# Where weight preparation, evictions and a few activations stand in the attention stretches of a two-block transformer kernel

## The chip, the cores and the metric

The kernel runs on one core of a Trainium2 chip. Its engines are TensorE (PE), VectorE (DVE), ScalarE (ACT), GpSimd (POOL) and the queue of SyncE (SP), which starts the weight loads. The metric is the device time of one execution in microseconds (us); lower is better.

## What is computed

A first block (gated sparse attention and forgetting attention on 256 tokens, merge, output, a gated embedding) and then two layers, each with a token mixer, attention over a memory of 256 rows, and a squared-ReLU MLP. All is float32. Cut to what matters:

```
proj = rmsnorm(x, g_pre) @ w_in                      # 256 x 3792, split into q, k, v, gates, indexer
att_a = dsa_branch(...)                              # indexer scores, top 64 keys, softmax
log_f = log_sigmoid(fb + b_forget)                   # the forget gate
att_b = fox_branch(qb, kb, vb, log_f)                # 8 heads, causal
out = (m_a * (att_a*silu(gate_a)) @ w_a + m_b * (att_b*silu(gate_b)) @ w_b) @ w_out
for i in range(2):                                   # layer 0: pool mixer, layer 1: MoBA mixer
    h = rms_norm(x) @ (w_in_pool if i == 0 else w_in_moba)
    tok = pool_mixer(h) if i == 0 else moba_mixer(h) # 12 heads, q and k normed per head and rotated
    mo = mem_cross_attention(h[..., -256:], mem_n)   # 4 heads
    x = x + concat(tok, mo) @ w_out[i]
    x = x + square(relu(rms_norm(x) @ w_ff1[i])) @ w_ff2[i]
```

With 256 tokens and blocks of 256 the MoBA mixer is plain causal attention.

## The kernel before

**Weights.** Every weight matrix is cut into units of 4 k-tiles of 128 rows by 512 columns (440 or 384 in the first projection), numbered through the program: `U_IN`, `U_MERGE`, ..., `U_POOL`, `U_OUT0`, `U_FF0`, `U_MOBA0`, `U_MOBA`, `U_OUT1`, `U_FF1`. I write POOL+5 for unit `U_POOL + 5`, MOBA+3 for `U_MOBA + 3`; `U_OUT1` is `U_MOBA + 8`. A unit is loaded by SP into one of two `raw` slots (four in the first projection); ACT rounds it into `w_hi` and DVE subtracts to get `w_lo` (L690 and L1090), both in a ring of four. The call `unit(u)` on ACT and on DVE prepares unit u + 3: ACT waits for its load and until PE has used unit u - 1. SP starts the load of unit v when `w_lo` of unit v - 2 is there.

**Products.** `product` (L1618) takes three matmuls for each k-tile and each of two token tiles (hi with hi, hi with lo, lo with hi), 24 for a whole unit; a k-tile is six. Two units make a block of 512 output columns in two PSUM banks. When both are done, `evac` copies the banks out, tile 0 on ACT and tile 1 on DVE (`block_done` is the wait for PE). The next block in the same banks waits for both copies (`banks_free`).

**Attention.** It is cut into steps n; each handles a pair of heads, the first four steps the indexer. Run 1 (steps 0 to 11, drained in 12 and 13) is the first block, which I call stage 1; run 2 (steps 12 and 13) is the memory attention of layer 0, stage 2; run 3 (steps 14 to 21, drained in 22 and 23) that of layer 1: two pairs of memory heads and six pairs of MoBA heads, stage 3. In step n PE does the scores of pair n (`logits`, L1760), transposes q and k of pair n + 1 (`qk_parts`, L1730), multiplies the values of pair n - 2 (`values`, L1814), then runs a piece of a dense product (`fill_of(n)`: a unit, two units or some k-tiles of one), then transposes the probabilities of pair n - 1 (`transposes`). ACT copies q and k (`copy_qk`), takes exponentials (`exps`), copies outputs and probabilities, and prepares `w_hi`; DVE takes maxima, normalises, subtracts (`out_lo`), copies probabilities (`copy_pt`, L1292) and prepares `w_lo`. `qk_parts(n)` waits for DVE's `copy_pt(n - 3)`, since both use one bank. The scores of a pair's first tile reuse the bank of the pair before.

**Order.** Each engine's program is written out by hand and runs in that order; tables name what fills which step (`IN_FILL`, `MOBA_FILL`, `OUT_FILL`) and when the squares for the head norms are taken (`SQUARES_AT`). A unit that is divided over steps is prepared by `late_unit` at the end of a step. GpSimd rotates q0, k0, q1, k1, q2, k2 in this order, each after its squares (`head_squares`, L1151 and L1152, on DVE), and `qk_parts` of a MoBA pair waits for its q and k.

## Time and profile before

| | |
|---|---|
| median of 3 runs | 851.4 us (850.99 to 852.76) |
| profiled execution | 850.99 us, span 849.1 us |
| PE busy | 820.9 us, 97% of the span |
| PE weight loads | 702.2 us, 83% |
| DVE busy | 528.5 us, 62% |
| ACT busy | 423.6 us, 50% |
| POOL busy | 117.3 us, 14% |
| data read | 138.86 MB, 165 GB/s over the span |

The chain that ended last lies on PE for 89% of the span, 54% of it the products of L1618 and 22% those of the MLP's first half (L1942). PE's busy time counts overlapping matmuls and modelled ends, so its idle pieces are what to look for; the view of waits names the engine whose work ended each of them, or "issue" where no single releaser shows. The span is the time between the first and last instruction of the profiled run; 1.9 us of its time lie outside.

### The profile page before, as it was taken

What the parts mean: (1) busy time and instruction counts of PE and PEld (TensorE: products, weight loads), DVE (VectorE), ACT (ScalarE), POOL (GpSimd) and SP (SyncE); (2) the same over time, 40 slices, a digit from 0 to 9 for tenths busy, and PEclk for the clock granted to TensorE, in tenths of its full rate; (3) what the DMA queues carried; (4) which work ended last, traced back from release to release, by engine and by line L of the source; (5) the groups of instructions that cost most, each with busy time, mean ns of one, the idle gap of its engine ahead of it and who ended that gap; (6) DMA issues with size and microseconds to landing.
All of it is one profiled execution on the core that took longest, in us unless ns stands there. A gap on an engine that the chain in (4) does not pass through costs nothing.

```text
span 849.1 us, 11701 instructions
## 1 busy us (share of the span) xinstructions
PE 820.9 (97%) x4506; PEld 702.2 (83%) x4506; DVE 528.5 (62%) x655; ACT 423.6 (50%) x620; POOL 117.3 (14%) x143
## 2 busy tenths in 40 slices
PE   6999999999999999999999999997989899999998
PEld 6998977778878767899999998875657799999996
DVE  5546988767586766565554455779774655445542
ACT  6446656554755555454444434545574544444440
POOL 2600300000030410030000000099500100000000
PEclk9999999999999999999999999999999999999999
DMA  8851452245646532555555555462122455555531
GB/s 316 295 180 39 149 192 106 103 158 200 247 152 220 195 131 69 198 182 176 188 197 197 176 180 189 161 208 77 52 98 100 156 192 198 173 178 193 198 148 50
DMA packets 76181, 140.42 MB, mean 165 GB/s; under 512 B 2888, under 2 KB 22544, under 8 KB 76144
## 3 DMA queue, kind: packets, MB, share of 16 engines
q1 hardware_dynamic: 74048, 134.03, 46.1%
q0 software_dynamic: 1936, 5.82, 2.0%
q8 instruction: 25, 0.41, 0.2%
q14 instruction: 12, 0.10, 0.0%
q10 hardware_dynamic: 160, 0.07, 0.0%
HBM read 138.86 MB, written 1.05 MB: 165 GB/s over the span
## 4 chain that ended last, share of the span: by engine, by line
PE 89%; ACT 4%; DVE 3%; issue 2%; DMA 1%; POOL 0%; SPq 0%; ACTq 0%; DVEq 0%
PE bank L1618 54%; PE bank L1942 22%; PE bank L1760 3%; PE bank L1678 2%; ACT w_hi L690 2%; PE bank L1814 2%; PE bank L1647 1%; DVE w_lo L1090 1%; PE bank L1730 1%; PE bank L1815 1%; PE bank L1632 1%; PE bank L1989 1%; PE bank L1790 1%; DMA raw<-in_w_ff 1%; DMA x<-in_x 1%
## 5 line engine op out<-in xcount | busy, mean ns | idle before, releaser
L1090 DVE TENSOR_TENSOR w_lo<-raw,w_hi 128x2048 fp32r<-128x2048 f32 (+2 forms) x69 | 155.3, 2254 | 63.3 <-ACT w_hi L690 62.9
L1495 DVE TENSOR_TENSOR w_lo<-raw,w_hi 128x2048 fp32r<-128x2048 f32 x48 | 110.2, 2295 | 91.6 <-ACT w_hi L1001 91.6
L690 ACT ACTIVATE w_hi<-raw 128x2048 fp32r<-128x2048 f32 (+2 forms) x69 | 129.9, 1884 | 67.1 <-PE bank L1618 41.6
L1618 PE MATMUL bank<-w_hi,b_hi 128*128 128x512 f32 x376 | 149.2, 397 | 0.1
L1618 PE MATMUL bank<-w_hi,a_hi 128*128 128x512 f32 (+2 forms) x376 | 146.9, 391 | 0.4 <-PE bank L1618 0.4
L1942 PE MATMUL bank<-a_hi,w_hi 128*128 128x256 f32 x512 | 145.4, 284 | 1.7 <-ACT tok L979 1.1
L1618 PE MATMUL bank<-w_lo,b_hi 128*128 128x512 f32 x376 | 146.6, 390 | 0.0
L1618 PE MATMUL bank<-w_hi,b_lo 128*128 128x512 f32 x376 | 146.5, 390 | 0.0
L1942 PE MATMUL bank<-a_lo,w_hi 128*128 128x256 f32 x512 | 144.9, 283 | 0.0
L1942 PE MATMUL bank<-a_hi,w_lo 128*128 128x256 f32 x512 | 144.9, 283 | 0.0
L1618 PE MATMUL bank<-w_hi,a_lo 128*128 128x512 f32 (+2 forms) x376 | 142.1, 378 | 0.0
L1618 PE MATMUL bank<-w_lo,a_hi 128*128 128x512 f32 (+2 forms) x376 | 141.7, 377 | 0.0
L1001 ACT ACTIVATE w_hi<-raw 128x2048 fp32r<-128x2048 f32 x48 | 92.2, 1922 | 98.5 <-PE bank L1618 64.7
L1942 PEld LDWEIGHTS bank<-a_hi,w_hi 128*128 128x128 f32 x512 | 98.2, 192 | 2.9 <-DVE w_lo L1090 1.5
L1942 PEld LDWEIGHTS bank<-a_lo,w_hi 128*128 128x128 f32 x512 | 98.2, 192 | 0.5
L1942 PEld LDWEIGHTS bank<-a_hi,w_lo 128*128 128x128 f32 x512 | 98.2, 192 | 0.0
L1618 PEld LDWEIGHTS bank<-w_hi,b_lo 128*128 128x128 f32 x376 | 70.6, 188 | 15.0
L1618 PEld LDWEIGHTS bank<-w_hi,b_hi 128*128 128x128 f32 x376 | 70.7, 188 | 14.2 <-DVE b_lo L1481 0.5
L1618 PEld LDWEIGHTS bank<-w_lo,b_hi 128*128 128x128 f32 x376 | 70.7, 188 | 13.5
L1618 PEld LDWEIGHTS bank<-w_hi,a_hi 128*128 128x128 f32 x376 | 70.7, 188 | 11.4 <-issue 1.8
L1618 PEld LDWEIGHTS bank<-w_hi,a_lo 128*128 128x128 f32 x376 | 70.6, 188 | 11.3
L1618 PEld LDWEIGHTS bank<-w_lo,a_hi 128*128 128x128 f32 x376 | 70.8, 188 | 10.5 <-issue 0.7
(244 smaller groups left out, 908.6 us busy)
## 6 DMA issues: line engine op xcount, KB each, us to landing
raw<-in_w_ff SPq DMA_DIRECT2D x64, 1024.0 KB, 5.1
raw<-in_w_in_moba SPq DMA_DIRECT2D x20, 512.0 KB, 4.3
raw<-in_w_merge SPq DMA_DIRECT2D x8, 1024.0 KB, 5.1
raw<-in_w_out SPq DMA_DIRECT2D x8, 1024.0 KB, 5.1
raw<-in_w_in SPq DMA_DIRECT2D x6, 880.0 KB, 7.5
m<-in_w_in SPq DMA_DIRECT2D x6, 880.0 KB, 7.1
raw<-in_w_mem_kv SPq DMA_DIRECT2D x4, 1024.0 KB, 5.2
raw<-in_w_ple_gate SPq DMA_DIRECT2D x4, 1024.0 KB, 4.9
```

The lines of the kernel that those rows point to most:

```text
L690: act.activation(w_hi[:, slot, 0:n], landing[land][:, 0:n], ACT.Copy).then_inc(hi_ready, 1)
L1001: act.activation(w_hi[:, (base + c) % RING, :], raw[:, (base + c) % RAW, :], ACT.Copy)\
L1090: dve.tensor_tensor(w_lo[:, v % RING, 0:n], landing[land_slot(v)][:, 0:n], w_hi[:, v % RING, 0:n].bitcast(F32), ALU.subtract).then_inc(lo_ ...
L1495: dve.tensor_tensor(w_lo[:, (base + c) % RING, :], raw[:, (base + c) % RAW, :], w_hi[:, (base + c) % RING, :].bitcast(F32), ALU.subtract). ...
L1618: ins = pe.matmul(banks[t][:, 0:n], xa[:, kt, ts], wa[:, slot, w], start=first and k == 0 and q == 0, stop=last and k == kts - 1 and q == 2)
L1632: ins = pe.matmul(banks[t][:, :], xa[:, k0 + k, ts], wa[:, u % RING, w], start=False, stop=k == 3 and q == 2)
L1647: ins = pe.matmul(banks[t][:, 0:n], xa[:, k0 + k, t * P:t * P + P], wa[:, u, k * n:k * n + n], start=k0 + k + q == 0, stop=k0 + k == D // ...
L1678: ins = pe.transpose(ps[:, kk * S + t * P:kk * S + t * P + P], src[:, t, (k + kk) * P:(k + kk) * P + P], ident[:])
L1730: ins = pe.transpose(b_io[:, i * S + t * P:i * S + t * P + P], cols[what][:, t], ident[:])
L1760: ins = pe.matmul(out, qT[:, t * P:t * P + P], k_of(n)[:, :, 0:w], start=True, stop=open_)
L1814: pe.matmul(out, v[:, 0], pT[0], start=True, stop=False)
L1942: ins = pe.matmul(b_hid[f][:, 0:S], wa[:, slot, w], xa[:, 4 * half_ + k, :], start=half_ + k + q == 0, stop=half_ == 1 and k == 3 and q == 2)
```

## The change

It moves work and adds or removes none. (1) In stage 1 the forget gate's Exp and Ln, and the dummy Exp that brings the table of Exp back, go from the ends of steps 0 and 2 to step 1, ahead of its unit. (2) On DVE a step's unit is now always prepared before the eviction of the block that the step ends; it was the other way for the second unit of a step and in stage 3. (3) In stage 2 units POOL+5 and POOL+6 are prepared before the two query copies (ACT) and before the first maxima (DVE), and PE's transposes and scores go in one k-tile earlier. (4) In stage 3 the dense part ends with MOBA+2, and the fills of steps 14 to 19 are MOBA+3 to MOBA+7 instead of MOBA+4 to MOBA+7; the squares of k1, q2 and k2 move with them. (5) `late_unit` prepares for a divided unit in the first of its steps, not in the last.

```
--- before.py
+++ after.py
@@ -146,7 +146,7 @@
     if n in BR_FILL:
         return [(U_BR + BR_FILL[n], B_BR + BR_FILL[n], 2, range(4))]
     if n in MOBA_FILL:
-        return [unit_of(U_MOBA + 4, B_MOBA + 2, *MOBA_FILL[n])]
+        return [unit_of(U_MOBA + 2, B_MOBA + 1, *MOBA_FILL[n])]
     if n in OUT_FILL:
         return [(U_OUT1, B_OUT1, 0, range(OUT_FILL[n], OUT_FILL[n] + 1))]
     return []
@@ -156,10 +156,10 @@
 MERGE_FILL = {6: (0, 1), 7: (2, 3), 8: (4,), 9: (5,), 10: (6,), 11: (7,)}
 BR_FILL = {12: 0, 13: 1}
 DRAIN = (12, 13, 22, 23)
-MOBA_FILL = {14: (0,), 15: (1,), 16: (2, range(0, 2)), 17: (2, range(2, 4)), 18: (3, range(0, 2)), 19: (3, range(2, 4))}
+MOBA_FILL = {14: (1,), 15: (2,), 16: (3,), 17: (4,), 18: (5, range(0, 2)), 19: (5, range(2, 4))}
 OUT_FILL = {20: 0, 21: 1, 22: 2, 23: 3}
 
-SQUARES_AT = {16: (("k2", B_MOBA + 2),)}
+SQUARES_AT = {15: (("k1", B_MOBA + 1), ("q2", B_MOBA + 1)), 17: (("k2", B_MOBA + 2),)}
 
 MOBA_BLOCKS = [(0, 3), (1, 9), (2, 4), (5, 6), (7, 8)]
 MOBA_AT = {piece: 256 * n for n, piece in enumerate(q for b in MOBA_BLOCKS for q in b)}
@@ -778,7 +778,7 @@
             def late_unit(n):
 
                 for u, k, half_, ks in fill_of(n):
-                    if 3 in ks and len(ks) < 4:
+                    if 0 in ks and len(ks) < 4:
                         unit(u)
 
             def copy_qk(n):
@@ -852,21 +852,20 @@
                     copy_qk(n + 1)
                 if n in run:
                     relus(n) if n < N_IDX else exps(n)
+                if n == 1:
+
+                    act.wait_ge(f_abs, 1)
+                    act.activation(fgt[:, 2], fgt[:, 1], ACT.Exp).then_inc(act_chain, 1)
+                    act.wait_ge(act_chain, 1)
+                    act.activation(fgt[:, 3], fgt[:, 2], ACT.Ln, bias=1.0).then_inc(f_ln, 1)
+
+                    act.activation(nmx[:, 0, 0, :], fgt[:, 1, 0, 0:2], ACT.Exp)
                 if gate_at(n) is not None:
                     gate_tanh(gate_at(n))
                 if n - 2 in run and n - 2 >= N_IDX:
                     out_hi(n - 2)
                 if n <= run[-1]:
                     fill(n)
-                if n == 0:
-
-                    act.wait_ge(f_abs, 1)
-                    act.activation(fgt[:, 2], fgt[:, 1], ACT.Exp).then_inc(act_chain, 1)
-                    act.wait_ge(act_chain, 1)
-                    act.activation(fgt[:, 3], fgt[:, 2], ACT.Ln, bias=1.0).then_inc(f_ln, 1)
-                if n == 2:
-
-                    act.activation(nmx[:, 0, 0, :], fgt[:, 1, 0, 0:2], ACT.Exp)
                 if n - 1 in run and n - 1 >= N_IDX:
                     copy_pt(n - 1)
                 late_unit(n)
@@ -1026,16 +1025,16 @@
                    .then_inc(d_copied_a, 1)
 
             first, second = RUN2
+            unit(U_POOL + 2)
             copy_qk(first)
+            unit(U_POOL + 3)
             copy_qk(second)
             exps(first)
-            unit(U_POOL + 2)
             block_done(U_POOL + 3)
             evac(B_POOL + 1)
             copy_pt(first)
             exps(second)
             copy_d(0)
-            unit(U_POOL + 3)
             out_hi(first)
             copy_d(1)
             copy_pt(second)
@@ -1062,10 +1061,7 @@
             block_done(U_MOBA + 1)
             evac(B_MOBA)
             unit(U_MOBA + 2)
-            unit(U_MOBA + 3)
             copy_qk(RUN3[0])
-            block_done(U_MOBA + 3)
-            evac(B_MOBA + 1)
             for n in steps_of(RUN3):
                 step(RUN3, n)
             for r in range(1, 4):
@@ -1160,22 +1156,18 @@
 
             def fill(n):
                 for i, (u, k, half_, ks) in enumerate(fill_of(n)):
-                    evicts = half_ and 3 in ks and BLOCKS[k] != "merge"
-                    late = i or n in RUN3
-                    if len(ks) == 4 and n not in DRAIN and not late:
-                        unit(u)
-                    if evicts:
-                        block_done(u)
-                        evac(k)
-                    if len(ks) == 4 and n not in DRAIN and late:
+                    if len(ks) == 4 and n not in DRAIN:
                         unit(u)
                     if i == 0 and n in RUN1 and kind_of(n) == "fox":
                         select_round(2 * (n - N_IDX) + 1)
+                    if half_ and 3 in ks and BLOCKS[k] != "merge":
+                        block_done(u)
+                        evac(k)
 
             def late_unit(n):
 
                 for u, k, half_, ks in fill_of(n):
-                    if 3 in ks and len(ks) < 4:
+                    if 0 in ks and len(ks) < 4:
                         unit(u)
 
             def add_half(c, b, r=None):
@@ -1542,9 +1534,10 @@
                 ins.then_inc(y_made, 1)
 
             first, second = RUN2
+            unit(U_POOL + 2)
+            unit(U_POOL + 3)
             maxima(first)
             normalise(first)
-            unit(U_POOL + 2)
             block_done(U_POOL + 3)
             evac(B_POOL + 1)
             copy_pt(first)
@@ -1554,7 +1547,6 @@
             out_lo(first)
             copy_d(1)
             copy_pt(second)
-            unit(U_POOL + 3)
             dve.wait_ge(pool_landed, 16 * 7)
             scale_mixed(0)
             group(G_TOK0, b_hi, b_lo, 0)
@@ -1578,9 +1570,7 @@
             dense(U_MOBA, B_MOBA)
             head_squares("memq1", B_MOBA)
             head_squares("q1", B_MOBA)
-            dense(U_MOBA + 2, B_MOBA + 1)
-            head_squares("k1", B_MOBA + 1)
-            head_squares("q2", B_MOBA + 1)
+            unit(U_MOBA + 2)
             for n in steps_of(RUN3):
                 step(RUN3, n)
             unit(U_OUT1 + 1)
@@ -1994,9 +1984,9 @@
             first, second = RUN2
             banks_free(B_POOL + 1)
             product(U_POOL + 2, (U_POOL + 2) % RING, a_hi, a_lo, 0, banks_of(B_POOL + 1), True, False,
-                    mid={3: lambda: qk_parts(first)})
+                    mid={2: lambda: qk_parts(first)})
             product(U_POOL + 3, (U_POOL + 3) % RING, a_hi, a_lo, 4, banks_of(B_POOL + 1), False, True,
-                    mid={1: both(lambda: logits(first), lambda: qk_parts(second)), 3: lambda: logits(second)})
+                    mid={0: both(lambda: logits(first), lambda: qk_parts(second)), 3: lambda: logits(second)})
             transposes(first)
             blocks_read(B_POOL + 1)
             pe.wait_ge(pool_landed, 16 * 7)
@@ -2021,7 +2011,9 @@
 
             dense(U_MOBA0, B_MOBA0, a_hi, a_lo, upper(G_MIX1, x, x_half, X_FF0 + 2))
             dense(U_MOBA, B_MOBA, a_hi, a_lo)
-            dense(U_MOBA + 2, B_MOBA + 1, a_hi, a_lo, ((), {1: lambda: qk_parts(RUN3[0])}))
+            banks_free(B_MOBA + 1)
+            product(U_MOBA + 2, (U_MOBA + 2) % RING, a_hi, a_lo, 0, banks_of(B_MOBA + 1), True, False,
+                    mid={2: lambda: qk_parts(RUN3[0])})
             for n in steps_of(RUN3):
                 step(RUN3, n)
             u = U_OUT1 + 1
```

In stage 1 the order on ACT from the end of step 0 to step 2, before (fgt is the forget gate, nmx the dummy's target, `prob` and `tok` the relus' targets, `w_hi<-m` units 14 and 15):

```order
L690 ACTIVATE w_hi<-raw 128x1536 [waits unit_used,raw_landed1]
L864 ACTIVATE fgt<-fgt 128x16 [waits f_abs]
L866 ACT_TABLE_LOAD
L866 ACTIVATE fgt<-fgt 128x16 [waits act_chain]
L791 ACTIVATE qT<-bank 128x256 [waits qk_tr]
L804 ACTIVATE tok<-bank 128x256 [waits s_ready]
L804 ACTIVATE tok<-bank 128x512 [waits s_ready]
L690 ACTIVATE w_hi<-m 128x1536 [waits unit_used,raw_landed2]
L739 ACTIVATE proj<-bank,stat 128x440 [waits rstd_done,unit_used]
L791 ACTIVATE qT<-bank 128x256 [waits qk_tr]
L804 ACTIVATE prob<-bank 128x256 [waits s_ready,idx_acc]
```

and after the change:

```order
L791 ACTIVATE qT<-bank 128x256 [waits qk_tr]
L804 ACTIVATE tok<-bank 128x256 [waits s_ready]
L804 ACTIVATE tok<-bank 128x512 [waits s_ready]
L858 ACTIVATE fgt<-fgt 128x16 [waits f_abs]
L860 ACT_TABLE_LOAD
L860 ACTIVATE fgt<-fgt 128x16 [waits act_chain]
L862 ACT_TABLE_LOAD
L862 ACTIVATE nmx<-fgt 128x2
L690 ACTIVATE w_hi<-m 128x1536 [waits unit_used,raw_landed2]
L739 ACTIVATE proj<-bank,stat 128x440 [waits rstd_done,unit_used]
L791 ACTIVATE qT<-bank 128x256 [waits qk_tr]
```

The five instructions on fgt and nmx now stand between the relus of step 1 and `w_hi` of unit 14, ahead of the eviction `proj<-bank`; the second table load used to stand behind the `w_hi` of step 2.

In stage 2 the order on ACT from the `w_hi` of POOL+4 on, before (qT and k_own are the query and key copies, prob the exponentials of the first pair):

```order
L690 ACTIVATE w_hi<-raw 128x2048 [waits unit_used,raw_landed1]
L789 ACTIVATE qT<-bank,gain_cols 128x256 [waits qk_tr]
L794 ACTIVATE k_own<-bank 64x256 [waits zeros_made]
L795 ACTIVATE k_own<-bank 64x256
L789 ACTIVATE qT<-bank,gain_cols 128x256 [waits qk_tr]
L794 ACTIVATE k_own<-bank 64x256 [waits zeros_made]
L795 ACTIVATE k_own<-bank 64x256
L817 ACTIVATE prob,psums<-bank,nmx,hstat 128x256 [waits max_done,pt_ready]
L817 ACTIVATE prob,psums<-bank,nmx,hstat 128x256
L817 ACTIVATE prob,psums<-bank,nmx,hstat 128x256 [waits max_done]
L817 ACTIVATE prob,psums<-bank,nmx,hstat 128x256
L690 ACTIVATE w_hi<-raw 128x2048 [waits unit_used,raw_landed0]
```

and after the change:

```order
L690 ACTIVATE w_hi<-raw 128x2048 [waits unit_used,raw_landed1]
L690 ACTIVATE w_hi<-raw 128x2048 [waits unit_used,raw_landed0]
L789 ACTIVATE qT<-bank,gain_cols 128x256 [waits qk_tr]
L794 ACTIVATE k_own<-bank 64x256 [waits zeros_made]
L795 ACTIVATE k_own<-bank 64x256
L690 ACTIVATE w_hi<-raw 128x2048 [waits unit_used,raw_landed1]
L789 ACTIVATE qT<-bank,gain_cols 128x256 [waits qk_tr]
L794 ACTIVATE k_own<-bank 64x256 [waits zeros_made]
L795 ACTIVATE k_own<-bank 64x256
L817 ACTIVATE prob,psums<-bank,nmx,hstat 128x256 [waits max_done,pt_ready]
L817 ACTIVATE prob,psums<-bank,nmx,hstat 128x256
L817 ACTIVATE prob,psums<-bank,nmx,hstat 128x256 [waits max_done]
```

The `w_hi` of POOL+5 stands before the first copy and that of POOL+6 before the second; before, the first of them came behind the exponentials.

In stage 3 the order on DVE from the normalisation of pair 15 to the copy of pair 14's probabilities (L1292), before (`proj<-bank` is the eviction of the block of MOBA+4 and MOBA+5):

```order
L1247 RECIPROCAL prec<-psums 128x2 [waits exp_done]
L1250 TENSOR_SCALAR tok<-tok,prec 128x256 [waits vec_chain]
L1250 TENSOR_SCALAR tok<-tok,prec 128x256
L1247 RECIPROCAL prec<-psums 128x2 [waits exp_done]
L1250 TENSOR_SCALAR tok<-tok,prec 128x256 [waits vec_chain]
L1250 TENSOR_SCALAR tok<-tok,prec 128x256
L1117 TENSOR_SCALAR proj<-bank,stat 128x512 [waits rstd_done,unit_used]
L1090 TENSOR_TENSOR w_lo<-raw,w_hi 128x2048 [waits hi_ready]
L1292 COPY probT<-bank 128x512 [waits pt_ready]
```

and after the change (line numbers are eight lower; m and hstat are the squares of k1 and q2):

```order
L1239 RECIPROCAL prec<-psums 128x2 [waits exp_done]
L1242 TENSOR_SCALAR tok<-tok,prec 128x256 [waits vec_chain]
L1242 TENSOR_SCALAR tok<-tok,prec 128x256
L1239 RECIPROCAL prec<-psums 128x2 [waits exp_done]
L1242 TENSOR_SCALAR tok<-tok,prec 128x256 [waits vec_chain]
L1242 TENSOR_SCALAR tok<-tok,prec 128x256
L1147 TENSOR_TENSOR m<-proj 128x512 [waits head_sum,banks_free_v,banks_free_a]
L1148 TENSOR_REDUCE hstat<-m 128x8 [waits vec_chain]
L1147 TENSOR_TENSOR m<-proj 128x512 [waits head_sum,banks_free_v,banks_free_a]
L1148 TENSOR_REDUCE hstat<-m 128x8 [waits vec_chain]
L1086 TENSOR_TENSOR w_lo<-raw,w_hi 128x2048 [waits hi_ready]
L1284 COPY probT<-bank 128x512 [waits pt_ready]
```

The eviction is gone from this step, since its block ends a step later, and four instructions of squares, which stood ahead of step 14, come before `w_lo` and the copy.

## Rows read from the trace of the kernel before

**Rows 1.** PE's waits in stage 1 (who waited <- for whom: total us, times, longest)

```profile
PE bank L1730 <- issue: 1.1, 1, 1.1
```

**Rows 2.** PE's waits from 285 to 360 us, around stage 2

```profile
PE bank L1981 <- issue: 1.6, 1, 1.6
PE bank L1989 <- DVE proj L1533: 0.4, 1, 0.4
```

**Rows 3.** PE's waits from 589 to 665 us, in stage 3

```profile
PE bank L1730 <- issue: 6.4, 3, 5.1
PE bank L1678 <- DVE x L1186: 2.4, 1, 2.4
PE bank L1814 <- DVE probT L1292: 1.9, 2, 1.5
PE bank L1760 <- ACT prob L817: 1.2, 1, 1.2
PE bank L1942 <- DVE a_lo L1102: 0.5, 1, 0.5
```

**Rows 4.** One stretch: busy time by engine, granted clock, DMA share, GB/s

```profile
594.50:598.00 3.50, 3.49 (x9) 1.95 (x9) 1.46 (x6) 2.38 (x9) 3.34 (x3) 0.51 0.74 256
```

**Rows 5.** ACT in order of time, stage 1 (start, length, what, [idle before])

```profile
66.37 1.28 ACT L866 ACT_TABLE_LOAD   x1
...
69.93 1.50 ACT L690 ACTIVATE w_hi<-m 128x1536 fp32r<-128x1536 f32 x1
...
77.76 1.28 ACT L869 ACT_TABLE_LOAD   x1
```

**Rows 6.** DVE in order of time, step 1 of stage 1

```profile
71.72 1.76 DVE L1090 TENSOR_TENSOR w_lo<-m,w_hi 128x1536 fp32r<-128x1536 f32 x1
73.71 0.68 DVE L1117 TENSOR_SCALAR proj<-bank,stat 128x440 f32<-128x440 f32 x1 [0.23 <-PE bank L1618]
```

**Rows 7.** The chain that ended last, stage 1 (start, length, what)

```profile
75.18 4.16 PE bank L1618 x24
```

**Rows 8.** Stretches of 1 us in stage 2, columns as in rows 4

```profile
302.00:303.00 1.00, 1.00 (x8) 0.86 (x7) 1.00 (x1) 0.60 (x2) 1.00 (x1) 1.00 0.97 369
...
307.00:308.00 1.00, 1.00 (x7) 0.86 (x6) 0.75 (x2) 0.66 (x2) 0.00 (x0) 1.00 0.44 170
```

**Rows 9.** ACT in stage 3: the `w_hi` of a late unit

```profile
624.76 1.91 ACT L690 ACTIVATE w_hi<-raw 128x2048 fp32r<-128x2048 f32 x1
```

**Rows 10.** ACT in stage 2: the first query copy and an exponential

```profile
302.40 0.48 ACT L789 ACTIVATE qT<-bank,gain_cols 128x256 f32<-128x256 f32 x1 [2.03 <-PE bank L1730]
...
308.49 0.56 ACT L817 ACTIVATE prob<-bank,nmx,hstat 128x256 f32<-128x256 f32 x1
```

**Rows 11.** The chain that ended last, in stage 2 and at the start of stage 3

```profile
302.36 2.78 PE bank L1618 x12
...
571.72 1.72 PE bank L1760 x4
```

**Rows 12.** DVE in stage 2: a maximum, a pair of normalise operations

```profile
306.04 0.69 DVE L1232 TENSOR_REDUCE mx<-bank 128x2 f32<-128x512 f32 x1 [3.00 <-PE bank L1760]
...
319.32 0.62 DVE L1250 TENSOR_SCALAR tok<-tok,prec 128x256 f32<-128x256 f32 x2
```

**Rows 13.** DVE in stage 3: a square, normalising pair 14, copying its probabilities

```profile
572.60 1.55 DVE L1151 TENSOR_TENSOR m<-proj 128x512 f32<-128x512 f32 x1
...
579.34 2.18 DVE L1250 TENSOR_SCALAR prob<-prob,prec 128x256 f32<-128x256 f32 x2
...
593.74 0.68 DVE L1292 COPY probT<-bank 128x512 f32<-128x512 f32 x1
```

**Rows 14.** DVE in stage 3: the copy behind the late unit

```profile
633.34 0.42 DVE L1292 COPY probT<-bank 128x256 f32<-128x256 f32 x1
```

**Rows 15.** The chain that ended last, late in stage 3

```profile
634.02 1.10 PE bank L1814 x2
...
637.59 1.38 PE bank L1618 x6
```

More of the change, by code:

```diff
@@ L148, in fill_of @@
     if n in MOBA_FILL:
-        return [unit_of(U_MOBA + 4, B_MOBA + 2, *MOBA_FILL[n])]
+        return [unit_of(U_MOBA + 2, B_MOBA + 1, *MOBA_FILL[n])]
     if n in OUT_FILL:
@@ L158 @@
 DRAIN = (12, 13, 22, 23)
-MOBA_FILL = {14: (0,), 15: (1,), 16: (2, range(0, 2)), 17: (2, range(2, 4)), 18: (3, range(0, 2)), 19: (3, range(2, 4))}
+MOBA_FILL = {14: (1,), 15: (2,), 16: (3,), 17: (4,), 18: (5, range(0, 2)), 19: (5, range(2, 4))}
 OUT_FILL = {20: 0, 21: 1, 22: 2, 23: 3}
-SQUARES_AT = {16: (("k2", B_MOBA + 2),)}
+SQUARES_AT = {15: (("k1", B_MOBA + 1), ("q2", B_MOBA + 1)), 17: (("k2", B_MOBA + 2),)}
 MOBA_BLOCKS = [(0, 3), (1, 9), (2, 4), (5, 6), (7, 8)]
@@ L780, in late_unit @@
                 for u, k, half_, ks in fill_of(n):
-                    if 3 in ks and len(ks) < 4:
+                    if 0 in ks and len(ks) < 4:
                         unit(u)
@@ L854, in step @@
                     relus(n) if n < N_IDX else exps(n)
+                if n == 1:
+                    act.wait_ge(f_abs, 1)
+                    act.activation(fgt[:, 2], fgt[:, 1], ACT.Exp).then_inc(act_chain, 1)
+                    act.wait_ge(act_chain, 1)
+                    act.activation(fgt[:, 3], fgt[:, 2], ACT.Ln, bias=1.0).then_inc(f_ln, 1)
+                    act.activation(nmx[:, 0, 0, :], fgt[:, 1, 0, 0:2], ACT.Exp)
                 if gate_at(n) is not None:
@@ L860, in step @@
                     fill(n)
-                if n == 0:
-                    act.wait_ge(f_abs, 1)
-                    act.activation(fgt[:, 2], fgt[:, 1], ACT.Exp).then_inc(act_chain, 1)
-                    act.wait_ge(act_chain, 1)
-                    act.activation(fgt[:, 3], fgt[:, 2], ACT.Ln, bias=1.0).then_inc(f_ln, 1)
-                if n == 2:
-                    act.activation(nmx[:, 0, 0, :], fgt[:, 1, 0, 0:2], ACT.Exp)
                 if n - 1 in run and n - 1 >= N_IDX:
@@ L1028, in _ @@
             first, second = RUN2
+            unit(U_POOL + 2)
             copy_qk(first)
+            unit(U_POOL + 3)
             copy_qk(second)
             exps(first)
-            unit(U_POOL + 2)
             block_done(U_POOL + 3)
@@ L1037, in _ @@
             copy_d(0)
-            unit(U_POOL + 3)
             out_hi(first)
@@ L1064, in _ @@
             unit(U_MOBA + 2)
-            unit(U_MOBA + 3)
             copy_qk(RUN3[0])
-            block_done(U_MOBA + 3)
-            evac(B_MOBA + 1)
             for n in steps_of(RUN3):
@@ L1162, in fill @@
                 for i, (u, k, half_, ks) in enumerate(fill_of(n)):
-                    evicts = half_ and 3 in ks and BLOCKS[k] != "merge"
-                    late = i or n in RUN3
-                    if len(ks) == 4 and n not in DRAIN and not late:
-                        unit(u)
-                    if evicts:
-                        block_done(u)
-                        evac(k)
-                    if len(ks) == 4 and n not in DRAIN and late:
+                    if len(ks) == 4 and n not in DRAIN:
                         unit(u)
@@ L1173, in fill @@
                         select_round(2 * (n - N_IDX) + 1)
+                    if half_ and 3 in ks and BLOCKS[k] != "merge":
+                        block_done(u)
+                        evac(k)
             def late_unit(n):
                 for u, k, half_, ks in fill_of(n):
-                    if 3 in ks and len(ks) < 4:
+                    if 0 in ks and len(ks) < 4:
                         unit(u)
@@ L1544, in _ @@
             first, second = RUN2
+            unit(U_POOL + 2)
+            unit(U_POOL + 3)
             maxima(first)
             normalise(first)
-            unit(U_POOL + 2)
             block_done(U_POOL + 3)
@@ L1556, in _ @@
             copy_pt(second)
-            unit(U_POOL + 3)
             dve.wait_ge(pool_landed, 16 * 7)
@@ L1580, in _ @@
             head_squares("q1", B_MOBA)
-            dense(U_MOBA + 2, B_MOBA + 1)
-            head_squares("k1", B_MOBA + 1)
-            head_squares("q2", B_MOBA + 1)
+            unit(U_MOBA + 2)
             for n in steps_of(RUN3):
@@ L1996, in _ @@
             product(U_POOL + 2, (U_POOL + 2) % RING, a_hi, a_lo, 0, banks_of(B_POOL + 1), True, False,
-                    mid={3: lambda: qk_parts(first)})
+                    mid={2: lambda: qk_parts(first)})
             product(U_POOL + 3, (U_POOL + 3) % RING, a_hi, a_lo, 4, banks_of(B_POOL + 1), False, True,
-                    mid={1: both(lambda: logits(first), lambda: qk_parts(second)), 3: lambda: logits(second)})
+                    mid={0: both(lambda: logits(first), lambda: qk_parts(second)), 3: lambda: logits(second)})
             transposes(first)
@@ L2023, in _ @@
             dense(U_MOBA, B_MOBA, a_hi, a_lo)
-            dense(U_MOBA + 2, B_MOBA + 1, a_hi, a_lo, ((), {1: lambda: qk_parts(RUN3[0])}))
+            banks_free(B_MOBA + 1)
+            product(U_MOBA + 2, (U_MOBA + 2) % RING, a_hi, a_lo, 0, banks_of(B_MOBA + 1), True, False,
+                    mid={2: lambda: qk_parts(RUN3[0])})
             for n in steps_of(RUN3):
```

## The prediction

> **What bounds the kernel now.** TensorE (PE) has the same matmuls before and after and is almost never without one, so I account in its idle time: the new time is the old one plus the change in PE's idle, plus what a slow clock adds. I read PE's waits stretch by stretch. They leave three places that the diff touches. In stage 1 (the first block's attention) PE idles 1.1 us behind VectorE's queue [rows 1]. In stage 2 (memory attention of the pool layer) it idles 1.6 and 0.4 us [rows 2]. In stage 3 (memory and MoBA attention of the second layer) it idles 12.4 us: 6.4 before query transposes (5.1 of it in one piece), 2.4 before the MLP's first transposes, 1.9 before `values`, 1.2 before a score matmul, 0.5 before the MLP [rows 3]. Right behind the 5.1 us piece the granted clock is 0.51 for 3.5 us [rows 4], the 1.2 GHz level for nearly all of it; half speed for 3.5 us costs some 1.8 us of work, so stage 3 loses about 14.2. The MLPs and the other dense blocks run without a break that matters, and the change doesn't touch them.
>
> **Part 1, the forget gate's activations (stage 1).** Exp, table load and Ln leave the end of step 0, a table load with a dummy Exp leaves the end of step 2; all five now stand in step 1, ahead of that step's weight unit. At their old places they cost nothing, because ScalarE waited for PE there. In step 1 they come between the relus and `w_hi` of unit 14. Their length is two loads of 1.28 [rows 5] and three activations of at most 16 columns, an estimate of 0.2 each since 1536 columns take 1.5: with gaps 3.3 us. `w_hi`, which ran from 69.9 for 1.5 us, then runs from 73.2 to 74.7. VectorE's `w_lo` (1.76) waits for it and ends at 76.5; only behind it comes `evac` of input block 5 (0.68), which ends at 77.2 instead of 74.4 [rows 6]. All blocks from 5 on use banks 0 and 1, so step 2's unit, whose first matmul stood at 75.2 [rows 7], waits for that eviction until 77.3: **2.1 us of new idle**. Nothing covers it; the old cover was 0.8 us, from the eviction's end to the matmul. The bounds are 0.3, if ScalarE's own eviction (0.6 long behind `w_hi`) were the last one waited for, and 2.8 without any cover.
> The Trainium skill, "ScalarE: Activation LUTs", section "Table sets: the hidden batching unit", says that one set holds ln and exp both, so that Ln and then Exp would need one load. Here each has its own load [rows 5], and the changed kernel's order has both too; by the page's rule the new idle would be about 0.8.
> The second effect: in steps 4 and 5 VectorE runs the second unit's `w_lo` before the eviction, not after it. Up to the copy of transposed probabilities that PE's 1.1 us waits for [rows 1], step 5's work is only permuted, so that the copy gains only what VectorE had idled before the evictions. Between 0 and 1.1 I take 0.4, since ScalarE's queue ahead of the `w_lo`s is no shorter. Stage 1: **+1.7 us**.
>
> **Part 2, stage 2.** The `w_hi`s of units POOL+5 and POOL+6 move in front of the two query copies, their `w_lo`s in front of the first maxima. They ran where they waited for nothing; now they wait for their loads, which stay where they were (each starts when the `w_lo` of two units earlier is done, and those don't move). The DMA engines are busy until about 303.0 for the first and 307.5 for the second [rows 8]. So the first `w_hi` runs 303.1 to 305.0 (1.9, [rows 9]) and the first copy 305.0 to 306.1 (three operations, 1.1 us together; it stood at 302.4 [rows 10]). PE reaches the first scores when unit POOL+2 is done, at 302.36 + 1.39 = 303.75 [rows 11], and waits until 306.3: **2.5 us**. The second `w_hi` runs 307.6 to 309.5 and its `w_lo` to 311.8 (2.3, from 1.76 for 1536 columns [rows 6]); then a maximum (0.85, [rows 12]) and two exponentials (0.56 each, [rows 10]): the first tile is done at 313.8. The second scores use the first ones' bank and stand after k-tile 2: 306.3 + 1.7 + 0.45 + 3 x 1.39 = 312.6, so **1.4 us** until 314.0. The rest brings PE to the pooling matmuls at 318.05; it began them at 315.7. The copies behind shift likewise, but ScalarE no longer has a `w_hi` among them, so the 0.4 us before `mixed` goes. Stage 2: 2.5 + 1.4 + 0.1 − 2.0 = **+2.0 us**. With the first load landed 1 us earlier it is +1.0, with 1 us later +3.0. Earlier weights buy nothing: no other wait stands in this stretch [rows 2].
>
> **Part 3, stage 3.** Unit MOBA+3 leaves the dense part and is step 14's fill; the next ones follow, steps 16 and 17 have whole units, 18 and 19 halves. The squares of k1 and q2 move from before step 14 to step 15, those of k2 from 16 to 17; `w_lo` precedes the eviction; the weight work of a divided unit moves from its last step (17, 19, 23) to its first (18, 20).
> *Steps 14 to 16.* VectorE is the late engine: it comes to the copy that PE's 5.1 us waits for at 593.7 [rows 13]. In the new order step 14's scores stand one unit (5.5) before 571.7 [rows 11], at 566.2. With transposes 0.44, unit 3 and scores 15 of 1.7, PE is through at 576.0. VectorE: maxima 14 at 567.1, normalise behind the exponentials until 574, `w_lo` to 576.2, eviction to 576.9. PE's next unit needs that eviction: **1.1 us of new idle**. Then maxima 15 to 578.6, normalise to 582.3, two squares to 585.8, `w_lo` to 588, copy to 588.6. PE is there at 584.9 and waits **3.8 us**, not 5.1. The lengths depend on something that I can't fix: a pair of normalise operations took 2.2 us here and 0.6 in stage 2, a square's multiply 1.55 here [rows 12, 13]. With all long the wait is 5.0, with all short about 1.
> *Late part.* A late weight unit puts `w_hi`, `w_lo`, maxima, exponentials, normalise, `out_lo` and copy in a row: from 624.8 [rows 9] to 633.8 [rows 14], 9.0 us, and 0.5 of copy ahead. Before, that stood behind step 19 and cost 1.2 + 1.5. Now it stands twice. Behind step 18 the eviction adds 0.7, against some 8.1 us of PE's own (half a unit 2.8, two scores 3.0, values 1.3, two small transposes): with the small waits around it 2.1. Behind step 20 only k-tiles are left: `values`, k-tile, transposes, k-tile are 4.9 us, from 634.0 to 639.0 [rows 15], and the scores 1.5: 9.5 + 0.2 − 6.4 = 3.3. With 0.4 and 0.2 of small ones: **6.0 us**, before 4.4.
> *Behind it.* `w_lo` of OUT1+3 comes some 16 us earlier, and with it the load of FF1+1, so the 2.4 us before the MLP's transposes [rows 3] go to 0; 0.5 stays.
> Sum: 1.1 + 3.8 + 6.0 + 0.5 = 11.4 against 12.4, and if no piece is long enough to lower the clock, the 1.8 go too. Stage 3: **−2.8 us**.
>
> **Sum.** +1.7 + 2.0 − 2.8 = +0.9 on a span of 849.1 gives 850.0; the profiled run has 1.9 around its span (850.99), so 851.9; the median of the runs shown is 0.4 above it: **852.3 us**. A measurement of this kernel tells about 0.2% from no change, 1.7 us, so this is inside "same" (849.7 to 853.1) and near its upper edge.
>
> **Rivals.**
> (A) *The clock falls after the 3.8 us wait as after the 5.1.* For it: that case [rows 4]. Against: the 2.4 us piece was followed by full speed, and 3.8 lies between. Price 1.8: 854.1. The Trainium skill, "TensorE: Matmul & The Clock Gate", section "HAM oscillation — how this bites in real kernels", says that idle gaps beyond a certain length lower the clock; the trace agrees for 5.1 us.
> (B) *VectorE is as slow in step 15 as it was in step 14* (normalise 2.2 a pair, squares 2.3): the wait stays 5.0 and the clock falls, +1.2 + 1.8: 855.3.
> (C) *The moved table loads are not what PE waits for*: ScalarE's eviction is, and 2.1 becomes 0.3, so 850.5.
> (D) *Faster.* VectorE's operations in steps 14 and 15 take their short lengths: the wait of 3.8 falls to 1 and the bank wait of 1.1 goes, 852.3 − 3.9 = 848.4. The sign turns when more than 2.6 us come out of VectorE's chain.
>
> **Chances.** Forecast 0.43 (own range 851.0 to 853.8), A 0.19, B 0.12, C 0.16, D 0.10. Slower by over 0.2%: most of A, all of B, the upper fifth of the forecast: 0.37. Faster: D: 0.10. Same: 0.53. The range leaves out most of D and the end of B: 849.3 to 855.3.
>
> **What would show it.** Right: a PE wait of 2 us before step 2's first weight matmul; waits of 2.5 and 1.4 us before the scores in stage 2; one of 3 to 4 us behind step 16's scores and full speed after it; 3.3 us before `values` near the end; none before the MLP's transposes. Wrong: without the first, part 1 falls; if the first copy in stage 2 keeps its time, part 2 falls; if the longest wait of stage 3 is under 1 us, D is the case.

## The result, and the profile after

The changed kernel takes 858.54 us (median of 7 runs, 854.95 to 860.05) against 851.3 us (median of 7, 849.53 to 852.76) before: a ratio of 1.0086 with a 95% interval of 1.007 to 1.0101. It is slower by 0.9%, 3.2 us beyond the upper end of the forecast range. The profiled execution took 859.29 us, with a span of 857.5 us. Two executions of later kernels, one of 1787 us and one of 1176 us, lie far off the rest and stand in no ratio.

I cut both traces at four matmuls: the first scores of step 0, the first `values` of pair 11, and the first matmul of either MLP. First the kernel before, then the changed one (start, length, what, [idle before]):

```profile
60.89 0.59 PE L1760 MATMUL bank<-k_shared,qT 128*128 128x256 f32 x2
...
189.12 0.59 PE L1814 MATMUL bank<-probT,x 128*128 128x512 f32 x1
...
355.14 0.28 PE L1942 MATMUL bank<-a_hi,w_hi 128*128 128x256 f32 x1
...
664.68 0.36 PE L1942 MATMUL bank<-a_hi,w_hi 128*128 128x256 f32 x1 [0.54 <-DVE a_lo L1102]
```

```profile
59.39 0.59 PE L1750 MATMUL bank<-k_shared,qT 128*128 128x256 f32 x2
...
189.50 0.59 PE L1804 MATMUL bank<-probT,x 128*128 128x512 f32 x1
...
361.25 0.28 PE L1932 MATMUL bank<-a_hi,w_hi 128*128 128x256 f32 x1
...
671.82 0.36 PE L1932 MATMUL bank<-a_hi,w_hi 128*128 128x256 f32 x1 [0.54 <-DVE a_lo L1098]
```

That makes three stretches, each with one stage of the change in it (the first MLP and the dense blocks behind it are in the third): 128.23, 166.02 and 309.54 us before; 130.11, 171.75 and 310.57 after. So **+1.9, +5.7 and +1.0 us**, where I had forecast +1.7, +2.0 and −2.8. The opening was 1.5 us shorter in this execution; over the fourteen traces of this document it takes 59.3 to 61.3 us. Behind the third stretch the changed kernel takes 1.2 us more, all of it behind PE's last matmul: the last store of the output lands 3.2 us after its issue, where before it was 2.0 (what, KB, us to landing; before, then changed):

```profile
out_x<-x SPq DMA_DIRECT2D x1, 256.0 KB, 2.0
```

```profile
out_x<-x SPq DMA_DIRECT2D x1, 256.0 KB, 3.2
```

It is 2.0 in the kernel before and in the two variants of it below that leave VectorE's order in stage 1 alone, and 3.2 in the other eleven traces. So it seems to come with part 2 of the change; no run here shows why.

The waits of PE in the changed kernel, in stage 1, around stage 2, and in stage 3 (against [rows 1], [rows 2] and [rows 3]):

```profile
PE bank L1608 <- issue: 1.9, 1, 1.9
PE bank L1720 <- issue: 0.8, 1, 0.8
```

```profile
PE bank L1750 <- issue: 3.8, 1, 3.8
PE bank L1720 <- DVE proj L1113: 0.9, 1, 0.9
```

```profile
PE bank L1720 <- issue: 5.4, 3, 3.5
PE bank L1804 <- DVE probT L1284: 3.8, 2, 3.1
PE bank L1608 <- issue: 1.2, 1, 1.2
PE bank L1932 <- DVE a_lo L1098: 0.5, 1, 0.5
```

Stage 3 waits 10.9 us, 1.5 less than before, and the 2.4 us before the MLP's transposes are gone. The waits are close to what the forecast had. What it did not have is the clock. Three stretches of the changed kernel (columns as in [rows 4]: the first five pairs are the engines' busy time, then granted clock, DMA share, GB/s):

```profile
307.30:314.00 6.70, 5.06 (x10) 2.82 (x11) 4.11 (x2) 3.86 (x7) 0.00 (x0) 0.50 0.75 275
594.00:600.70 6.70, 5.76 (x12) 3.43 (x13) 4.74 (x13) 4.29 (x14) 6.26 (x7) 0.50 0.45 159
648.60:651.90 3.30, 3.30 (x12) 2.72 (x12) 1.27 (x3) 1.36 (x3) 0.00 (x0) 0.50 0.00 0
```

The clock is 0.50, the 1.2 GHz level, at and behind each of the three long waits (3.8, 3.5 and 3.1 us), where before it was so behind one [rows 4]. PE was busy in these stretches for 5.1, 5.8 and 3.3 us, so half, some 7.1 us of work, was lost to the clock instead of 1.8.

### The profile page after: what moved, and what is told of

It is laid out like the page before. It is cut to its first block, busy times and chain, and to the rows that moved or that the text cites. A ratio compares the mean times of both kernels' runs of the same rounds, so it can differ in the third digit from the quotient of the medians.

```text
span 857.5 us, 11703 instructions
## 1 busy us (share of the span) xinstructions
PE 825.3 (96%) x4506; PEld 703.9 (82%) x4506; DVE 527.1 (61%) x655; ACT 424.2 (49%) x620; POOL 114.4 (13%) x143
## 4 chain that ended last, share of the span: by engine, by line
PE 60%; DVE 2%; issue 1%; ACT 1%; ACTq 0%
PE bank L1608 31%; PE bank L1932 22%; PE bank L1750 2%; PE bank L1804 1%; DVE w_lo L1086 1%; PE bank L1668 1%; PE bank L1805 1%; PE bank L1622 1%; PE bank L1979 1%; PE bank L1720 1%; PE bank L1780 0%; PE bank L1971 0%; ACT w_hi L690 0%; PE bank L1786 0%; ACT tok L817 0%
```

## The experiments

All times are medians, all ratios against the kernel before on the same chip, with 95% intervals. A table of the three stretches of each profiled execution stands at the end of this section.

**Undoing one stage of the change at a time.** First stage 2 (ScalarE's part is shown; VectorE's units and PE's k-tiles go back too):

```
+            copy_qk(first)
+            copy_qk(second)
+            exps(first)
             unit(U_POOL + 2)
-            copy_qk(first)
-            unit(U_POOL + 3)
-            copy_qk(second)
-            exps(first)
...
             copy_d(0)
+            unit(U_POOL + 3)
```

> The changed kernel with part 3 of the change undone (units POOL+5 and POOL+6 prepared where they were before). Theory T: a long wait of PE costs its length and, where the granted clock falls to half for it, half of the low stretch that work falls in. In the trace after the change stage 2 waits 3.8 + 0.9 us (before 1.6 + 0.4) and then works 5.1 us at half clock, 2.55 us lost; PE reaches the first MLP 5.7 us later relative to the end of stage 1. So without part 3 the time should fall by 5.3 to 5.9 us from the changed kernel's, to about 852.8, and no half clock should stand between 300 and 320 us. Theory W (rival): the clock's fall there is an accident of the run or comes from elsewhere, part 3 costs its waits alone: the time falls by 2.7 us and a low stretch still shows up in this neighbourhood.

Measured: 854.24 us, ratio 1.0038 (1.0024 to 1.0051), where the changed kernel has 1.0086: 4.1 us come back, less than T expected (5.3 to 5.9) and more than W (2.7). Its trace has stage 2 exactly as before, 166.02 us, and no low clock there; two low stretches are left in stage 3. Part 3 of the change is the largest loss, and the low clock in stage 2 comes with it.

Stage 3 as before, stages 1 and 2 changed:

```
-MOBA_FILL = {14: (1,), 15: (2,), 16: (3,), 17: (4,), 18: (5, range(0, 2)), 19: (5, range(2, 4))}
+MOBA_FILL = {14: (0,), 15: (1,), 16: (2, range(0, 2)), 17: (2, range(2, 4)), 18: (3, range(0, 2)), 19: (3, range(2, 4))}
...
-                    if 0 in ks and len(ks) < 4:
+                    if 3 in ks and len(ks) < 4:
```

> The changed kernel with stage 3 as it was before (parts 4 and 5, and the order of eviction and weight work in stage 3), stages 1 and 2 changed. Theory T: from step 14 to the second MLP the changed kernel took 1.0 us more (waits 10.9 instead of 12.4 us, two half-clock stretches that lose 2.85 and 1.65 us instead of one that loses 1.8), so this kernel should be 1 us faster than the changed one, about 857.5, with one low stretch in stage 3 and the 5.1 us wait back. Theory W (waits alone): it should be 1.5 us slower than the changed kernel.

Measured: 859.96 us, 1.0097 (1.0078 to 1.0117), the same as the changed kernel within the intervals. T expected 857.5 and W 860.0, so by the time alone W did better. In its trace stage 3 is 0.5 us shorter than in the changed kernel and the low stretches are those that T counts on, but the clock fell once more, in a place where it had not fallen in the other traces, behind the 1.9 us wait of stage 1:

```profile
75.69 0.41 PE L1617 MATMUL bank<-w_hi,a_hi 128*128 128x384 f32 x1 [1.94 <-issue]
```

```profile
77.00:80.50 3.50, 3.50 (x13) 3.50 (x13) 2.04 (x5) 0.00 (x0) 0.00 (x0) 0.52 0.00 0
```

That doesn't explain the median: the profiled execution has a mean clock of 0.990, the five others have 0.992 and average 859.1 us. The miss of T here stays open.

Stage 1's activations at their old places (part 1 undone):

```
-                if n == 1:
+                if n == 0:
                     act.wait_ge(f_abs, 1)
...
+                if n == 2:
                     act.activation(nmx[:, 0, 0, :], fgt[:, 1, 0, 0:2], ACT.Exp)
```

> The changed kernel with part 1 undone (forget gate's activations back at the ends of steps 0 and 2). Both theories: the 1.9 us wait before step 2's weight matmuls goes, nothing comes for it, the clock stays full: 1.9 to 2.2 us faster than the changed kernel, about 856.4. A rival for stage 1 alone: the wait only moves to the 0.8 us one at step 5, then the gain is under 1 us.

Measured: 856.07 us, 1.0058 (1.0041 to 1.0075), 2.4 us less than the changed kernel; the wait is gone, and stage 1 takes 127.87 us, 2.2 less than changed and 0.4 less than before. That 0.4 is what part 2 brings there.

**Keeping PE busy in the waits.** This is the test of the clock. PE gets matmuls that nobody reads (fillers), ahead of the wait:

```
+            def filler(n, count):
+                pe.wait_ge(pt_cp_a, n - N_IDX + 1)
+                for _ in range(count):
+                    pe.matmul(b_t[:, :], a_hi[:, 0, 0:P], a_hi[:, 0:2, :], start=True, stop=True)
```

> The changed kernel, with extra matmuls on PE whose results nobody reads, in front of its three long waits: 14 ahead of the first scores of stage 2 (wait 3.8 us), 13 ahead of the query transposes in step 16 (3.5 us), 12 ahead of the values in step 22 (3.1 us), each a 128x512 product of some 0.2 us into the bank of the transposed probabilities. They fit into the waits, so they take no time of their own. Theory T: PE is not idle, the clock stays full, and the lost 2.55 + 2.85 + 1.65 = 7.05 us come back: about 851.5. Theory W: the low stretches have another cause (DMA traffic, what VectorE and GpSimd do at that time) and stay: 858.5 as the changed kernel, or up to 1 us more.

Measured: 857.35 us, 1.0071 (1.0053 to 1.0088). T expected 851.5, so this is a miss. It doesn't speak for W either: the low stretches at the first two places are gone. At the third, in step 22, the fillers themselves had to wait for ScalarE's copy and then ran past the end of the wait:

```profile
PE bank L1744 <- ACT probT L844: 2.2, 1, 2.2
```

So the same again, with a bank that is free at all three places:

```
+            def filler(pair, count):
+                pe.wait_ge(exp_done, 2 * pair + 2)
+                for _ in range(count):
+                    pe.matmul(b_s1[pair % 2][:, :], a_hi[:, 0, 0:P], a_hi[:, 0:2, :], start=True, stop=True)
```

> The changed kernel with the unread matmuls again, but written to a score bank that is free at all three places, so that none of them waits for ScalarE's copy of the transposed probabilities (in the first such kernel those of step 22 waited 2.2 us for it and then ran into PE's own time: 857.4 us at a granted clock of 1.00 but for one stretch). 14, 13 and 12 of them as before. Theory T (clock): stage 2 takes 3.4 us more than before the change instead of 5.7; from the first to the second MLP the low stretches go (4.5 us), but VectorE's queue, on which PE waits there, doesn't move with the clock, so that part of the 4.5 turns into longer waits: 1.5 to 4 us come back. In sum 4 to 6.5 us under the changed kernel, 852 to 854.5. Theory T' (the clock costs nothing where a queue of VectorE stands behind it): only stage 2's 2.3 us come back, 856. Theory W: 858.5.

Measured: 853.74 us, 1.0037 (1.0023 to 1.0052), as T said. The mean clock was 1.00 in five of its six executions (0.990 to 0.996 in those of the changed kernel), and its trace has no low stretch from 50 us to the last matmul. The fillers took nothing but idle time from PE, which still waited 0.4, 0.15 and 0.4 us behind them at the three places. So **4.2 to 4.8 us of the changed kernel's time is the clock**, by ratio and by median; between the two traces the three stretches differ by more, 6.7 us (2.3 in stage 2, 4.4 in stage 3), and the spans by 5.1, as the two openings differ by 1.7 the other way. Its waits around stage 2 show what the slow clock had covered:

```profile
PE bank L1760 <- ACT prob L817: 1.2, 1, 1.2
PE bank L1760 <- ACT k_own L795: 0.4, 1, 0.4
```

The first is the wait before the second scores, forecast at 1.4 us. In the changed kernel PE was too slow to arrive early, and it did not show. The second is what the first scores still wait behind the fillers.

**What a fall costs in the kernel before.** Sixteen such matmuls ahead of its 5.1 us wait:

> The kernel before with 16 unread matmuls in front of the 5.1 us wait in step 16 and nothing else. Theory T with the prediction's price: the half clock behind that wait goes and 1.8 us come back, 849.5. Theory T': PE works faster behind the wait, but comes to the next wait for VectorE's or ScalarE's queue all the sooner: under 0.8 us come back.

Measured: 851.84 us (851.1 without the execution of 1787), 1.001 (0.9997 to 1.0023): nothing comes back, as T' said. Nor does it where the clock was full throughout: three executions at a mean clock of 1.000 average 850.4 us, the kernel before beside them 850.0 at 0.998. In its trace (an execution of 854.8 us, the longest that counts) the first low stretch is gone, but the next wait before query transposes is 2.1 us instead of 0.3, and behind it, and behind the 2.4 us wait before the MLP's transposes, the clock fell at 604 and 662 us. That 2.4 us wait had left it full in the trace of before.

**Moving the copy.** One instruction of VectorE in the kernel before:

```
+                if n == 15:
+                    copy_pt(n - 1)
                 fill(n)
-                if n - 1 in run and n - 1 >= N_IDX:
+                if n - 1 in run and n - 1 >= N_IDX and n != 15:
                     copy_pt(n - 1)
```

> The kernel before with one instruction of VectorE moved: in step 15 it copies pair 14's transposed probabilities before it evicts and prepares the unit, not after. The copy then runs at 590.9 instead of 593.7. Theory T: the 5.1 us wait becomes 2.2, the clock stays full or nearly so: 2.9 us of waiting and up to 1.8 of the clock come back, less what turns up behind: 847 to 848.5. If the later waits of stage 3 are set by VectorE's queue from further ahead (T'), they grow by what the copy saved, and under 1 us comes back.

Measured: 849.43 us, 0.9995 (0.9977 to 1.0013), unclear. The 5.1 us wait became 2.0, but 0.3 became 2.2 in the next step, since the queue of VectorE is as long as it was: of the 3.1 us saved 1.9 came back, as T' has it. Its executions lie far apart, and with the clock: the three at a mean clock of 1.000 average 847.3 us, which is what T expected with a full clock, the two at 0.994 average 854.3.

**Part 5 undone** (the condition of `late_unit` alone, `3 in ks`):

> The changed kernel with part 5 undone: the weight work of a divided unit again at the end of its last step (19 and 23, not 18 and 20). Theory T: the 3.1 us wait before the values of step 22 and the low stretch behind it (3.3 us, 1.65 lost) go; a shorter wait of about 1.5 us comes behind step 19, and the 2.4 us wait before the second MLP's transposes is back. In sum 1 to 2 us under the changed kernel, 857. The prediction's part 5 alone: -1.6 for the late part, +2.4 at the MLP, so 0.8 us over it.

Measured: 858.17 us, 1.0095 (1.0079 to 1.011), no difference from the changed kernel; expected was 857. The 3.1 us wait and the low stretch behind it are gone, and 1.2, 1.5 and 2.7 us are there instead. Part 5 trades waits at even terms.

**The parts that the forecast counted as gains**, without parts 1 and 3:

> The kernel before with parts 2, 4 and 5 of the change and without parts 1 and 3, so all of what the prediction counted as a gain. By the stretches of the traces so far: stage 1 takes 0.4 us less (as in the changed kernel without part 1), stage 2 is as before, stage 3 takes 0.3 to 1.0 us more, since two low stretches of the clock eat what the shorter waits bring. T: within 1 us of the kernel before, 851.5. The prediction's own working gives -0.4 - 2.8, so 848.2.

Measured: 851.36 us, 1.0008 (0.9995 to 1.0021): no gain, as T said and the prediction did not. The trace has low stretches behind the 3.5 and the 3.1 us wait:

```profile
587.00:593.00 6.00, 5.50 (x11) 3.26 (x12) 4.04 (x12) 4.03 (x14) 5.56 (x7) 0.50 0.48 175
642.00:644.00 2.00, 2.00 (x9) 1.81 (x8) 1.27 (x3) 1.19 (x3) 0.00 (x0) 0.50 0.00 0
```

**A version that beats both.** The kernel before with the copy first in step 15, stage 1's order of part 2, and the divided output unit prepared in step 22, not 23:

```
-                    if 3 in ks and len(ks) < 4:
+                    if (2 if n in OUT_FILL else 3) in ks and len(ks) < 4:
```

> The kernel before with three changes of order: pair 14's probabilities copied ahead of step 15's eviction and weight work (wait 5.1 to 2.2 us), part 2's order in stage 1 (-0.4), and the weight work of the divided output unit in step 22 instead of 23, some 4 us earlier, so that the load that the 2.4 us wait before the MLP's transposes comes from starts earlier. No unread matmuls. T: waits fall by 2.9 + 0.3 + 2.4 us; where the clock stays full the time is about 844.5, where it falls once behind one of the waits about 846.5. By T' (VectorE's queue gives it back behind the copy) 849.

Measured: 846.36 us, **0.9955** (0.9941 to 0.9969): faster than both, and near where T put it with one fall (846.5). Stage 3's waits are 8.2 us instead of 12.4, the 2.4 before the MLP's transposes is not among them, none is over 2.2, and four of nine executions had a mean clock of 1.000:

```profile
PE bank L1732 <- issue: 4.6, 3, 2.2
PE bank L1816 <- DVE probT L1292: 1.9, 2, 1.5
PE bank L1762 <- ACT prob L817: 1.2, 1, 1.2
PE bank L1944 <- DVE a_lo L1102: 0.5, 1, 0.5
```

Those four average 845.8 us, 1.3 over the 844.5 that T gave for a full clock; the last store, which lands 1.2 us later here than in the kernel before, is in none of the expectations.

The same with fillers ahead of its four waits:

> The same kernel with unread matmuls ahead of four waits: 6 before the pooling matmuls (1.6 us), 8 before the query transposes of step 16 (2.2 us), 4 before the scores and 5 before the values of step 21 (1.2 and 1.5 us). T: the clock is full in every execution (1.00), so the spread of the times shrinks and the median is 1 to 2 us under that of the same kernel without them, 844 to 845. If the clock falls by chance whatever PE does, no difference.

Measured: 845.66 us, 0.995 (0.9927 to 0.9974), not to be told from the last. T expected a full clock in every execution, and that is a miss: it was full in four of seven (844.9 us on average); in the profiled one PE met a 3.1 us wait in step 17 that had no fillers, and the clock fell there.

Last, stage 3 of the change with the copy first and fillers for two waits:

> The kernel before with parts 2, 4 and 5 of the change, the copy of pair 14's probabilities first in step 15, and unread matmuls ahead of the waits of step 16 (5 of them) and step 22 (12). T: stage 1 -0.4; stage 3 by the trace with a full clock -3.4, and the 3.5 us wait becomes about 1.2, -2.3 more where nothing behind it takes it back: 845 to 847.5. If the wait for the copy comes back in the next step: 847.5.

Measured: 847.94 us, 0.997 (0.9958 to 0.9982), just above the upper end of 847.5. All eleven executions that count had a clock of 0.998 to 1.000: with the clock held and the copy first, stage 3 in the order of the change is 2.8 us shorter than before (the order of the best version, 5.7).

The three stretches of each profiled execution, in us (first scores to pair 11's `values`; to the first MLP; to the second):

| kernel | stage 1 | stage 2 | stage 3 | low clock at |
|---|---|---|---|---|
| before | 128.23 | 166.02 | 309.54 | 594 |
| changed | 130.11 | 171.75 | 310.57 | 307, 594, 648 |
| stage 2 as before | 130.08 | 166.02 | 309.84 | 591, 642 |
| stage 3 as before | 131.67 | 171.75 | 310.06 | 77, 309, 599 |
| stage 1 as before | 127.87 | 170.42 | 309.84 | 308, 591, 646 |
| fillers, first | 130.07 | 169.41 | 310.21 | 643 |
| fillers, second | 130.10 | 169.46 | 306.16 | none |
| before + filler | 128.22 | 166.05 | 313.53 | 604, 662 |
| before + copy first | 128.25 | 165.97 | 308.60 | 657 |
| part 5 undone | 130.06 | 170.63 | 310.87 | 308, 595 |
| parts 2, 4, 5 | 127.90 | 165.99 | 311.04 | 586, 641 |
| best | 127.88 | 166.03 | 303.85 | none |
| best + fillers | 127.90 | 166.00 | 307.31 | 601 |
| stage 3, copy, fillers | 127.92 | 165.96 | 306.74 | none |

## Why the prediction was wrong

Parts are numbered here as in the section on the change: part 3 is stage 2 (the prediction's "Part 2"), parts 4 and 5 are stage 3.

**Part 1 was right.** Forecast 2.1 us of idle before step 2's unit; measured 1.95. The order on ScalarE has both table loads, and `w_hi` behind them, then VectorE's `w_lo` and eviction:

```profile
68.68 1.28 ACT L860 ACT_TABLE_LOAD   x1
69.97 0.22 ACT L860 ACTIVATE fgt<-fgt 128x16 f32<-128x16 f32 x1
70.21 1.28 ACT L862 ACT_TABLE_LOAD   x1
...
71.61 1.47 ACT L690 ACTIVATE w_hi<-m 128x1536 fp32r<-128x1536 f32 x1
```

```profile
73.19 1.76 DVE L1086 TENSOR_TENSOR w_lo<-m,w_hi 128x1536 fp32r<-128x1536 f32 x1 [3.00 <-ACT w_hi L690]
74.86 0.67 DVE L1113 TENSOR_SCALAR proj<-bank,stat 128x440 f32<-128x440 f32 x1
```

```profile
75.63 0.41 PE L1608 MATMUL bank<-w_hi,a_hi 128*128 128x384 f32 x1 [1.95 <-issue]
```

The wait at PE's 1.1 us place became 0.8, the gain of part 2 was 0.4 as forecast: stage 1 came to +1.9 against +1.7. Rival C falls.

**Part 3 had the mechanism and too small a size.** ScalarE's first copy did wait behind a `w_hi` that waited for its load, and PE for the copy:

```profile
305.91 1.91 ACT L690 ACTIVATE w_hi<-raw 128x2048 fp32r<-128x2048 f32 x1 [4.77 <-DMA raw<-in_w_out]
307.73 0.46 ACT L789 ACTIVATE qT<-bank,gain_cols 128x256 f32<-128x256 f32 x1
```

But the load of POOL+5 was there at 305.9, not at 303.1 as the step had it from [rows 8]. Counted from pair 11's `values`, that is 116.4 us against 114.0; in the five other traces with this order it was 114.8 to 116.3. Some 0.6 of it is a misreading: the DMA engines' share falls at 303, but this load, issued at 298.7 in the trace of before, landed at 303.7, which is 114.6. The rest is spread. The load starts when the `w_lo` of POOL+3 is done, and the load of POOL+3 runs beside GpSimd's loads for the pooling; it took 10.15 us there and 12.0 here, and in that time the DMA engines, busy in both, moved 322 and 288 GB/s:

```profile
284.30:294.40 10.10, 10.10 (x50) 8.35 (x49) 7.49 (x12) 6.07 (x10) 5.92 (x10) 1.00 0.98 322
```

```profile
284.60:296.60 12.00, 12.00 (x58) 9.94 (x57) 7.55 (x12) 6.11 (x10) 6.60 (x10) 1.00 0.97 288
```

Of all fourteen traces the one I read has the earliest landing of POOL+3, 10.15 us after the issue where the others have 10.25 to 12.0; why it differs between executions is not shown. Before the change the load had slack, so its spread cost nothing; the change put PE behind it. With the clock kept full stage 2 takes +3.4 us, near the step's own "+3.0" for a load landed 1 us later (it was 1.2 later in that trace). The step gave that bound and then took the single value.

**Parts 4 and 5: the waits were right, and the conclusion was not.** Forecast 1.1, 3.8 and 6.0 us of waits and none before the MLP's transposes; measured 1.2, 3.5, and 0.96 + 0.96 + 0.66 + 3.14 = 5.7, and none. (The 1.1 is in part luck: the terms that should bring PE to 576.0 add up to 575.5.) With the clock kept full the third stretch is 3.4 us shorter than before, where the forecast had −2.8.

**The step that failed** is "if no piece is long enough to lower the clock, the 1.8 go too", and with it rival A, which priced one fall behind one wait and came to 854.1. B and D fall with the 3.5 us measured for their wait, and no rival reached 858.5. The forecast itself had put down a wait of 2.5 us in stage 2 and one of 3.3 late in stage 3, and asked of neither what the clock would do. I had one fall (5.1 us) and one wait without (2.4 us) and read them as a threshold in between. They are not: behind the same 2.4 us wait before the MLP's transposes the clock fell in two of these traces, and behind 1.9 us in one. With the clock kept full, the forecast's sum of +0.9 becomes +1.9 (1.9 + 3.4 − 3.4), inside the range. The last store adds 1.2, a term that the forecast did not have: together 3.1 us, which is the 1.0037 of the kernel with fillers. The low clock, 4.2 to 4.8 us, is the rest of the 7.2.

The Trainium skill, "TensorE: Matmul & The Clock Gate", section "HAM oscillation — how this bites in real kernels", says that idle gaps beyond a certain length lower the clock. The traces agree for the waits of 3.5 to 5.1 us. They differ for shorter ones, for which the page's rule would keep the clock full: the granted clock was 0.5 at or behind every wait of 3.1 and 3.2 us, and behind waits of 1.9 to 2.4 us in some traces and not in others.

**A second thing the forecast missed** was shown by the fillers in the kernel before: taking the low clock away there brought nothing (1.001). Where PE waits for VectorE's queue step after step, work that PE does sooner is work that it waits for longer. That reading is argued, and it does not carry over: in stage 2 of the changed kernel, where no such wait follows, the trace gets back 2.3 us of some 2.5 lost, but in its stage 3, where such waits do follow, 4.4 of some 4.5. What a fall costs has to be measured in the order at hand.

What stays open is what decides, for one wait, whether the clock falls and for how long (3.3 to 6.7 us in the rows above), and why the last store lands later.

## What to carry to other kernels

Price a new wait of TensorE twice, once as idle time and once for the clock, whenever it is some 2 us or longer, and do it for each wait in the forecast, not for the longest. Don't put an engine that others wait for behind a load that had slack, on the strength of one trace: read how late that load can be. And a chain that a second engine holds back can give nothing for a faster first one; move the one instruction that is waited for, then look at what the queue makes late next.

## What the runs showed of the hardware

- The clock fell in some executions and not in others behind one and the same wait: 1.9 us in step 2 (one trace with a fall, five without), 2.4 to 2.7 us before the MLP's transposes (two with, three without). At or behind each of the 16 waits of 3.1 to 5.1 us that had no fillers ahead, from the first scores on in all traces, it fell.
- The fall can come within the wait or behind it: the 3.8 us wait of the changed kernel ended at 308.94, and the clock was down at 307.3; its 3.1 us wait ended at 647.48, and the clock was full until 648.5.
- The kernel before itself runs at different mean clocks: of 27 executions beside the last experiments 14 had 0.998 and averaged 849.7 us, 7 had 0.996 and 850.9, 6 had 0.994 and 851.8.
- Matmuls that nobody reads, 2.9 to 3.3 us of them at each of three long waits, held the granted clock at 1.00 in the second kernel with fillers.
- A weight load of 1 MB beside loads of another queue took 10.15 to 12.0 us over the fourteen traces, and the last store of 256 KB 2.0 us in three of them and 3.2 in eleven.
